# First layer's h tile by tile, table loads placed by hand, a spare PSUM bank for attention's first turns, and a feed-forward that starts in halves

## The reference

```python
c_act = silu(c)
for l in range(2):                                   # first block
    mod = c_act @ w_ada[l] + b_ada[l]                # 6 x 1024 values: shifts, scales, gates
    h = rms_norm(x, g_pre_mix[l]) * (1 + sc_mix) + sh_mix
    y = mixer(h, ...)                                # w_in, two causal convolutions, mLSTM heads, group norms, w_out
    x = x + gt_mix * rms_norm(y, g_post_mix[l])
    h = rms_norm(x, g_pre_mlp[l]) * (1 + sc_mlp) + sh_mlp
    f = square(relu(h @ w_ff1[l])) @ w_ff2[l]        # 1024 -> 4096 -> 1024
    x = x + gt_mlp * rms_norm(f, g_post_mlp[l])
# second block: projections of rms_norm(x), pooling, sparse attention of 16 heads (compressed,
# selected and window branch, softmax with a bias), cross attention to a memory, a gated merge,
# and a feed-forward that gathers the top 16 of 16384 experts for each of 8 heads and 256 tokens
```

## Time and profile before

| | |
|---|---|
| median of 3 runs | 2131.85 us (2130.0 to 2132.73) |
| the profiled execution | 2135.83 us, its span 2134.1 us |
| mean granted TensorE clock | 0.974 |
| TensorE busy | 1939.1 us (91%) |
| VectorE, ScalarE, GpSimd busy | 1052.3, 497.0, 319.6 us |
| DMA | 517.38 MB, mean 242 GB/s |
| first dense matmul starts | 35.78 us |

### The profile page before, as it was taken

The page is one execution under the profiler, slowest core; times in us unless marked ns, Lnnn a source line. Parts: engine busy times, 40 slices in busy tenths (PEclk is TensorE's granted clock), DMA queues, the critical chain, the costliest instruction groups (busy, mean ns, idle before and its releaser), DMA issues.

```text
span 2134.1 us, 20902 instructions
## 1 busy us (share of the span) xinstructions
PE 1939.1 (91%) x7920; PEld 1423.8 (67%) x7920; DVE 1052.3 (49%) x2563; ACT 497.0 (23%) x1205; POOL 319.6 (15%) x332
## 2 busy tenths in 40 slices
PE   4999899999999999999999999998887878887877
PEld 4876688888887788888889777786443433433333
DVE  6993466501597432000210323225767767767754
ACT  2123321101113322110100544312223223222223
POOL 1000001100000000000000000002444434444442
PEclk9999999999999999999999999999999999999899
DMA  9711079944351133448652222435999999999997
GB/s 401 289 59 60 21 314 371 397 161 155 139 199 68 73 144 141 153 154 179 249 183 80 109 79 79 188 128 235 401 422 422 421 421 409 421 421 421 421 422 291
DMA packets 71715, 517.38 MB, mean 242 GB/s; under 512 B 8128, under 2 KB 8384, under 8 KB 11456
## 3 DMA queue, kind: packets, MB, share of 16 engines
q0 software_dynamic: 46384, 330.85, 38.9%
q1 hardware_dynamic: 25232, 185.21, 22.9%
HBM read 510.78 MB, written 5.24 MB: 242 GB/s over the span
## 4 chain that ended last, share of the span: by engine, by line
PE 72%; DMA 15%; DVE 9%; ACT 3%; issue 1%; SPq 0%; another core or an unknown queue 0%; POOL 0%; DVEq 0%; ACTq 0%
PE pj L579 17%; DMA region<-in_peer_uv,small 12%; PE pj L784 9%; PE pj L799 9%; PE st L1052 8%; PE pj L731 5%; DVE region L1941 3%; PE pj L592 3%; PE pj L1021 2%; PE pj L623 1%; PE pj L828 1%; PE st L866 1%; PE pj L925 1%; DMA pe_T<-in_pe_cols 1%; DMA ring<-in_ring_w 1%
## 5 line engine op out<-in xcount | busy, mean ns | idle before, releaser
L1052 PE MATMUL st<-region 128*128 128x512 f32 x940 | 446.5, 627 | 113.1 <-ACT region L1402 112.9
L1052 PEld LDWEIGHTS st<-region 128*128 128x128 f32 x940 | 180.2, 198 | 371.7 <-issue 196.0
L579 PE MATMUL pj<-hT,ring 128*128 128x256 f32 x1760 | 384.1, 380 | 1.0 <-ACT region L1228 1.0
L579 PEld LDWEIGHTS pj<-hT,ring 128*128 128x128 f32 x1760 | 333.6, 190 | 47.4 <-ACT region L1228 1.8
L1941 DVE CUSTOM_DVE_ANT_0 region<-region 128x1024 f32<-128x1024 f32 x235 | 285.5, 1223 | 116.5 <-DMA region<-in_peer_uv,small 114.5
L497 POOL DMA_INDIRECT region<-in_peer_uv,small x235 | 256.3, 1091 | 398.1 <-PE st L1052 328.4
L784 PE MATMUL pj<-region,ring 128*128 128x256 f32 x1024 | 222.2, 379 | 4.1 <-ACT region L1228 2.7
L784 PEld LDWEIGHTS pj<-region,ring 128*128 128x128 f32 x1024 | 194.2, 190 | 32.4 <-ACT region L1228 3.5
L1560 DVE SCALAR_TENSOR_TENSOR region<-region,pc 128x255 f32<-128x255 f32 (+19 forms) x528 | 202.7, 467 | 0.0
L1512 DVE TENSOR_TENSOR tmp<-xT,hT 128x256 f32<-128x256 f32 x32 | 13.6, 425 | 366.4 <-ACT hT L1129 366.4
L1402 ACT ACTIVATE region<-ident,small 128x128 f32<-128x128 f32 x256 | 89.0, 394 | 377.5 <-DVE small L1949 377.5
(11 more groups left out here) (345 smaller groups left out, 2020.1 us busy)
## 6 DMA issues: line engine op xcount, KB each, us to landing
ring<-in_ring_w SPq DMA_DIRECT2D x157, 1024.0 KB, 4.9
region<-in_ada_rest POOLq DMA_DIRECT2D x40, 1024.0 KB, 12.4
region<-in_ada_first SPq DMA_DIRECT2D x4, 2048.0 KB, 17.6
region<-in_wqkv SPq DMA_DIRECT2D x2, 3072.0 KB, 12.3
region<-in_wcmp POOLq DMA_DIRECT2D x2, 2048.0 KB, 9.4
bias_dram<-region POOLq DMA_DIRECT2D x1, 4096.0 KB, 46.9
region<-in_w_o POOLq DMA_DIRECT2D x4, 1024.0 KB, 6.2
region<-in_peer_uv,small POOLq DMA_INDIRECT x235, 15.8
```

The lines of the kernel that those rows point to most:

```text
L579: i = nc.tensor.matmul(b[:, m, :], w[:, k, P * m:P * m + P], hT[:, k, :], start=(k == 0), stop=(k == CT - 1))
L1052: i = nc.tensor.matmul(acc[:, u % 2, 512 * hf:512 * hf + 512], diag[:, m % NDIAG, :], uv[m % NBUF][:, D + 512 * hf:D + 512 * hf + 512], st ...
```

## The change

- Modulation tiles 0 to 15 come as eight pairs (`PAIRS`; shift tile c with scale tile c), and SP issues them, x, the columns and the first four ring slots in the order `EARLY`. VectorE makes each tile of h of layer 0 as soon as its pair is there (`first_pair`, `first_h`). The sum of x's squares is formed over all partitions at once as a 128x256 row in `ms[1]`, whose root and reciprocal `x_rstd` replace the column, the diagonal and the spread. The first two projections run in `wide_first`: the first job a tile at a time, the second following from the third tile on. Four chunks of modulation leave their place before the convolutions: two go behind the last long convolution, one each into the first two heads, and `modulation(0, 16, 24)` behind the heads.
- Tables of ScalarE: dummy activations of one column load Sqrt, Sigmoid and, behind each of three drains between heads, Exp. In both layers the drain of the projection of index 11 (a Sigmoid) moves from before the four Silus to between the second and the third.
- In both layers four of the eight group sums of the long convolution run before the heads' spread, into the other half of `st`.
- The second feed-forward waits for the last drains of the first only at its second job.
- In attention the first turn of each unit goes to `ms[1]` (`spare`): that of the compressed branch, which came last, or in the "x" units the first of two. It has its own semaphore `spare_kept`.
- Some semaphores are joined under one name, and the late small parameters get one of their own (`params2_in`).

The diff, cut to its core (left out: the same layout change in `lay_out`, waits whose semaphore only has a new name, `load_layer`'s wait for `x_summed` in place of `x_spread`, and counters that start one lower or higher):

```diff
@@ -28,6 +28,8 @@
 ADA_FIRST = 16
+PAIRS = ADA_FIRST // 2
+EARLY = ["ada0", "x", "ada1", "cols", "ada2", "ring", "ada3", "ring", "ada4", "ada5", "ada6", "ada7", "ring", "ring"]
 ADA_BUFS = 4
@@ -375,12 +378,20 @@
             sp.dma_start(c_act, a["c"].partition_broadcast(P)).then_inc(sem("c_in"), 16)
-            sp.dma_start(xT[:, :, :], a["x_cols"]).then_inc(sem("x_in"), 16)
-            for j in range(4):
-                sp.dma_start(ada_first[:, j], a["ada_first"][j]).then_inc(sem(f"ada_first{j}"), 16)
-            sp.dma_start(pc[:, :, :], a["cols"]).then_inc(sem("params_in"), 16)
-            sp.dma_start(pc2[:, :], a["cols2"]).then_inc(sem("params_in"), 16)
-            sp.dma_start(pe_T[:, :, :], a["pe_cols"]).then_inc(sem("params_in"), 16)
+            n = 0
+            for what in EARLY:
+                if what == "x":
+                    sp.dma_start(xT[:, :, :], a["x_cols"]).then_inc(sem("x_in"), 16)
+                elif what == "cols":
+                    sp.dma_start(pc[:, :, :], a["cols"]).then_inc(sem("params_in"), 16)
+                elif what == "ring":
+                    sp.dma_start(ring[:, n, :], a["ring_w"][n]).then_inc(ring_full[n], 16)
+                    n += 1
+                else:
+                    j = int(what[3:])
+                    sp.dma_start(ada_first[:, j], a["ada_first"][j]).then_inc(sem(f"ada_first{j}"), 16)
+            sp.dma_start(pc2[:, :], a["cols2"]).then_inc(sem("params2_in"), 16)
+            sp.dma_start(pe_T[:, :, :], a["pe_cols"]).then_inc(sem("params2_in"), 16)
@@ -565,12 +578,14 @@
             pe.wait_ge(sem("consts"), 1)
-            for s in range(2):
-                for c in range(CT):
-                    pe.wait_ge(sem("x_squared"), c + 1)
-                    i = nc.tensor.matmul(ms[0][:, 0, s:s + 1], tmp[:, c, P * s:P * s + P], ones[:, 0:1], start=(c == 0), stop=(c == CT - 1))
+            for c in range(CT):
+                pe.wait_ge(sem("x_squared"), c + 1)
+                i = nc.tensor.matmul(ms[1][:, 0, :], ones[:, :], tmp[:, c, :], start=(c == 0), stop=(c == CT - 1))
             i.then_inc(sem("x_summed"), 1)
-            spread_x()
+            for c in range(CT):
+                for s in range(2):
+                    i = nc.tensor.matmul(ms[0][:, 0, CT * s + c:CT * s + c + 1], tmp[:, c, P * s:P * s + P], ones[:, 0:1], start=True, stop=True)
+            i.then_inc(sem("x_summed"), 1)
@@ -598,14 +613,36 @@
+            def wide_first(js):
+
+                banks = [take_bank(), take_bank()]
+
+                def step(n, k):
+                    w = ring_slot(("w_in", 0, js[n])).rearrange("p (k n) -> p k n", n=256)
+                    for m in range(2):
+                        i = nc.tensor.matmul(banks[n][:, m, :], w[:, k, P * m:P * m + P], hT[:, k, :], start=(k == 0 and m == 0), stop=(k == CT - 1 and m == 1))
+                    if k == CT - 1:
+                        i.then_inc(sem("slot_used"), 1)
+
+                for k in range(CT):
+                    pe.wait_ge(sem("h_ready"), k + 1)
+                    step(0, k)
+                    for late in ((), (), (0, 1), (2, 3))[k] if k < 4 else (k,):
+                        step(1, late)
+
             for l in range(DEPTH):
-                wide("w_in", l, W_IN_ORDER[:10], 16 * l)
+                if l == 0:
+                    wide_first(W_IN_ORDER[:2])
+                    wide("w_in", l, W_IN_ORDER[2:10])
+                else:
+                    wide("w_in", l, W_IN_ORDER[:10], 16 * l)
...
                 pe.wait_ge(sem("wg_in"), 48 * (l + 1))
+                pe.wait_ge(sem("x_sum_kept"), 1)
                 for c in range(2 * H):
@@ -711,6 +748,11 @@
                 i.then_inc(sem("var_made"), 1)
+                pe.wait_ge(sem("conv_ready"), 4 * (l + 1))
+                for c in range(4):
+                    i = nc.tensor.matmul(st[:, 4 + c, :], ones[:, :], U[:, 16 + c, :], start=True, stop=True)
+                    if c % 2:
+                        i.then_inc(sem("gn_summed"), 1)
                 if l:
...
-                pe.wait_ge(sem("conv_ready"), 4 * (l + 1))
-                for c in range(CT):
-                    i = nc.tensor.matmul(st[:, c, :], ones[:, :], U[:, 16 + c, :], start=True, stop=True)
+                for c in range(4, CT):
+                    i = nc.tensor.matmul(st[:, c - 4, :], ones[:, :], U[:, 16 + c, :], start=True, stop=True)
                     if c % 2:
@@ -764,7 +805,7 @@
                 wide("w_ff1", l, list(range(16)), 16 * l + 8)
-                pe.wait_ge(sem("proj_drained"), bank)
+                hidden = bank
                 for j in range(16):
...
                         nc.tensor.matmul(ms[1][0:NH, :, :].rearrange("p a t -> p (a t)"), rel[0:N_BUCKETS, :], onehot[0:N_BUCKETS, :],
-                                         start=True, stop=True).then_inc(sem("bias_made"), 1)
+                                         start=True, stop=True).then_inc(sem("mem_turned"), 1)
                     if j % 2 == 0:
                         b = take_bank()
+                    if j == 1:
+                        pe.wait_ge(sem("proj_drained"), hidden)
                     for k in range(16):
@@ -891,19 +934,19 @@
                 pb = probs[u % 2]
+                spare = ms[1].rearrange("p a t -> p (a t)")
                 pe.wait_ge(sem("probs_ready"), u + 1)
+                if g != "x":
+                    nb = NCMP if s else NCMP // 2
+                    for r in range(R):
+                        i = nc.tensor.transpose(spare[0:nb, P * r:P * r + P], pcmp[:, u % 2, r, 0:nb], ident[:, :])
+                    i.then_inc(sem("turned"), 1)
                 for m in range(1 if g == "x" else 2):
                     for j in range(2 if g == "x" else s + 1):
-                        b = take_bank().rearrange("p a t -> p (a t)")
+                        b = spare if g == "x" and j == 0 else take_bank().rearrange("p a t -> p (a t)")
                         for r in range(R):
...
                         i.then_inc(sem("turned"), 1)
-                if g != "x":
-                    nb = NCMP if s else NCMP // 2
-                    b = take_bank().rearrange("p a t -> p (a t)")
-                    for r in range(R):
-                        i = nc.tensor.transpose(b[0:nb, P * r:P * r + P], pcmp[:, u % 2, r, 0:nb], ident[:, :])
-                    i.then_inc(sem("turned"), 1)
@@ -1094,8 +1137,10 @@
             act.wait_ge(sem("consts"), 1)
-            std_x()
-            act.wait_ge(sem("params_in"), 48)
+            nc.scalar.activation(gsum[:, 0:1], eps_col[:, :], ACT.Sqrt)
+            act.wait_ge(sem("x_summed"), 1)
+            nc.scalar.activation(x_rstd, ms[1][:, 0, :], ACT.Sqrt, bias=eps_col[:, 0:1], scale=1.0 / D).then_inc(sem("x_std"), 1)
+            act.wait_ge(sem("params_in"), 16)
@@ -1145,6 +1190,8 @@
                 finish_h(l, 0)
+                if l == 0:
+                    nc.scalar.activation(gsum[:, 0:1], eps_col[:, :], ACT.Sigmoid)
                 if l:
...
                         drain(vtok[:, s, 512 * hp:512 * hp + 512].rearrange("p (a t) -> p a t", a=2), ACT.Copy)
-                drain_u(l, W_IN_ORDER[10:12])
+                drain_u(l, W_IN_ORDER[10:11])
                 for h in range(H):
...
                     nc.scalar.activation(xc[:, 2 * h:2 * h + 2, :], xc[:, 2 * h:2 * h + 2, :], ACT.Silu).then_inc(sem("xc_ready"), 1)
+                    if h == 1:
+                        drain_u(l, W_IN_ORDER[11:12])
                     if h:
@@ -1192,6 +1241,7 @@
                         drain_u(l, [5 + h])
+                        nc.scalar.activation(gsum[:, 0:1], eps_col[:, :], ACT.Exp)
@@ -1334,17 +1386,22 @@
                 keep_fill(FILL[u][0])
+                spare = ms[1].rearrange("p a t -> p (a t)")
+                if g != "x":
+                    turned += 1
+                    act.wait_ge(sem("turned"), turned)
+                    nc.scalar.copy(pcmpT[0:nb, :, :].rearrange("p r t -> p (r t)"), spare[0:nb, :]).then_inc(sem("spare_kept"), 1)
                 for m in range(1 if g == "x" else 2):
...
                         act.wait_ge(sem("turned"), turned)
-                        nc.scalar.copy(probsT[:, m, j].rearrange("p r t -> p (r t)"), pj[bank_of()][:, :, :].rearrange("p a t -> p (a t)")).then_inc(sem("proj_drained"), 1)
+                        dst = probsT[:, m, j].rearrange("p r t -> p (r t)")
+                        if g == "x" and j == 0:
+                            nc.scalar.copy(dst, spare).then_inc(sem("spare_kept"), 1)
+                            continue
+                        nc.scalar.copy(dst, pj[bank_of()][:, :, :].rearrange("p a t -> p (a t)")).then_inc(sem("proj_drained"), 1)
                         bank += 1
-                if g != "x":
-                    turned += 1
-                    act.wait_ge(sem("turned"), turned)
```

(62 more changed lines are left out.)

54 lines of the change are left out of this document (31 added, 23 removed).

## The result

The changed kernel takes 2118.22 us (median, 2116.9 to 2118.67), the kernel before in the same comparison 2132.22 us; the ratio is 0.9935, interval 0.9918 to 0.9953. That is 14.0 us faster, where 21.6 were forecast. Two further measurements of the same code gave 2118.91 us (ratio 0.994, 0.9923 to 0.9957) and 2116.59 us (0.9939, 0.992 to 0.9959).

What follows compares the result with a forecast made beforehand. It took TensorE, busy 91% of the span and 72% of the chain, as the bound. Terms of -8.6 -3.5 +0.9 +0.4 -3.7 -2.7 -4.4 gave -21.6 us: 2114.2 from the profiled 2135.83, 2110.3 as median; range 2104.5 to 2118.

Steps and rivals of the forecast that it cites:

- Start, -8.6: Kernel start: first two jobs end at 44.2 instead of 52.9 us, 8.6 us gained, bounds 5.3 to 10.5.
- rival 1: Start: short matmul bursts behind each h tile run at slow clock, 3.3 us back, 2113.6 us; chance 0.22.
- rival 2: Start: the first h chain holds more than seen, so it gains only about 1 us, 2118 us; chance 0.10.
- Silu, -3.5 and +0.9: Heads' q matmuls: earlier Silus gain 3.5 us in layer 0; a third-head stall costs 0.9 in layer 1.
- the 1.8 us that the sum has for the clock: Layer 0's q: part of the 3.5 us gain, for 64 records that ran in 15.61 us against 13.9.
- Exp's table, 0: Between heads: loading the exponential's table ahead gains nothing, bounds 0.3 us either way.
- Second feed-forward, -2.7: Turn between feed-forwards: TensorE's wait for the last tile's Relu and Square goes, 1.34 us in each layer.
- Group sums, -3.7: Norms: four sums fill layer 0's idle gap, 1.73 us, plus 2.0 from the clock; layer 1 gains 0.
- I take half of it, 2.0: Layer 0's norms: half of 4.0 us of slow clock at the spread and next 32 records is recovered.
- Attention, -4.4: Attention: each unit's first turn in a spare bank removes stalls, 4.4 us in all, bounds 2.5 and 5.5.
- rival 3: Attention gains nothing, as ScalarE's serial copies and the wait for spare_kept replace the stall: 2114.7 us; chance 0.13.
- Rival 4: Whole kernel: denser TensorE is granted less clock; 0.960 costs 22 us, 0.954 gives 2142 us; chance 0.02.

Runs made afterwards that it cites:

- delayed kernels: Changed kernel with VectorE clearing 512, 1024 or 2048 columns of h before SP's first transfer, so all starts later: 2118.69, 2119.86 and 2121.04 us.
- the second version: Changed kernel with x requested first, layer 1's old Silu order, useless matmuls in TensorE's gaps and full-width norm matmuls: 2108.6 us, ratio 0.989.
- the fillers: Changed kernel with 16 matmuls whose result nobody reads put into TensorE's gaps around layer 0's norms: 2112.29 us, ratio 0.991.

## Why the prediction came out as it did

The direction was right and the time was not: 2118.22 us lies above the likeliest 2110.3 and 0.2 us above the range. The steps, one by one:

- **Start, -8.6.** The two jobs end 10.0 us earlier in the first two profiles, and by the average of all five the projections end 9.4 earlier (98.7 against 108.2). The chain came as listed (root at 17.16, forecast 17.9; a tile of h every 3.20 us, forecast 3.3; eight records behind the last). The last bursts ran at full rate, so rival 1 does not hold, nor does rival 2. 
- **Silu, -3.5 and +0.9.** The stall at the third head is 0.90 us in both layers and 1.1 us with what follows. From the end of the projections to the gate sums layer 0 takes 43.0 us on average against 46.0: 3.0 gained of 3.5. In the first two profiles it is 1.6, since the 1.8 us that the sum has for the clock are not there: either profile holds two slow stretches in that stage, at 113 and 137 us before and both at 101 now. A table load of 1.28 us at 129.40 is followed by its activation at 130.69 here too, so the total for a switch that the prediction names from the Trainium skill, "ScalarE: Activation LUTs", section "What ACT_TABLE_LOAD costs", again overstates it.
- **Exp's table, 0.** 0.1 us a layer. Right.
- **Second feed-forward, -2.7.** The gap is gone in both layers, and putting it back costs 2.7 us in the stages. Right; the table's first feed-forward shows nothing because a third slow stretch stands there, at 306 or at 530 us.
- **Group sums, -3.7.** This is the step that failed most. "I take half of it, 2.0" counted on the clock. The filled gap gave its 1.7, the spread went to full clock (1.1), but the 32 records behind the remaining wait stayed slow (9.56), and a stretch that was not there before appeared at 248 us. In two of the three profiles a stretch at 213 also made the variance sums 1.5 to 1.7 us longer. Net -0.1 over the stage, between nothing and -1.1 for the edit alone. The 6.93 in the prediction is also a little low, as it leaves out the last record's tail that the 9.81 holds: the row for 32 records at full clock is 7.14 to 7.17, so the slow clock had 3.8 us and not 4.0. In layer 1 the "0" became +1.6 in the same way.
- **Attention, -4.4.** The edit gives 3.8; rival 3 does not hold. The profiles' stage gains only 1.0, since the changed kernel had four or five slow stretches there, the kernel before two or three. In the two delayed kernels with three, the stage takes 265.1 us, against 268.8 before with three: 3.8 again.

The failed step, then, is that the sum let the granted clock change only where an edit touched the code, and there for the better: it booked 1.8 us at q of layer 0 and 2.0 in the norms. Counted in the windows from 60 us to the merge, both profiles of the kernel before hold 17 slow stretches; the three of the changed kernel hold 20, 20 and 19, on average 2.7 more, which is 4.5 us (the three delayed ones 18, 18 and 20; with them it is 2.2 more, 3.7 us). The mean granted clocks of the executions point the same way: 0.970 to 0.978, median 0.972, in 12 of the changed kernel, against 0.974 to 0.983, median 0.979, in 38 of the kernel before. The 0.974 on which the prediction built lies at the lower end of these. So by the three profiles the clock took 4.5 us where the sum gave 3.8. With the 0.6 of attention and 0.3 of layer 1's stall, less 0.8 that the start gained beyond its term, that makes 8.4 against the 8.3 us by which the table's gain falls short; with five profiles behind it, so close an agreement is in part luck. Rival 4 had the outcome, a changed kernel that is granted less, but priced only its extreme, and its reason, that TensorE is denser, is not shown; a term of two or three stretches more, 3.4 to 5 us, was what the case wanted. The count of stretches as a whole is shown; which edit brought which of them is not, beyond what the experiments say.

**What of the stretches is settled.** Filling the waits brings the 32 records at 224 to 231 us back to full clock (shown). The moved group sums are not needed for the stretch in layer 1 (shown). Full-width matmuls in the norms remove both stretches behind the spreads: with them none is there at 2.6 and 2.3 us behind the beat, where the thin ones had one in every case from 2.4 on (one kernel; the second version has none either). The Trainium skill, "TensorE: Matmul & The Clock Gate", section "HAM oscillation — how this bites in real kernels", tells of matmuls so thin that TensorE waits for DMA between them and falls to the lower level; here the rows show a fall with no wait at all, so that page's mechanism is not this one. That the kernel before, with the same thin matmuls, has no stretch there, that the Silu order of layer 1, 120 us earlier, removes it, and that it is back when that order is joined with the fillers, all go with where the spread lies against the clock's beat (1.5, 1.3 and 1.2 us behind it). So thin matmuls make a fall possible, and their position seems to decide; a run that moves that position alone is missing.
